# Attention block: query tiles ahead of the maxima on VectorE, sink columns written a step sooner, and W_o's tiles shared out as 12, 12, 18 and 6 matmuls over the last four steps

## The chip, the cores and the metric

The kernel runs on one core of a Trainium2 chip. The metric is the device time of one execution in microseconds. Before the change it is 1058.06 us, the median of three runs (1057.86 to 1059.98).

## What is computed

A two-layer decoder trunk in float32 on one sequence of 512 tokens and width 1024: an S5 layer with its MLP, then one attention layer with its MLP, and a final RMSNorm. The change touches only the attention layer: 16 query heads over 4 shared K/V heads, causal window of 128, and one learned sink logit for each head.

```python
s = einsum(q, k) / sqrt(64);  s = where(band, s, -inf)      # per block of 128 queries, 256 keys
m = maximum(max(s), sink)
p = exp(s - m);  denom = sum(p) + exp(sink - m)
o = einsum(p / denom, v)
h = h + o @ w_o + b_o
```

## The kernel before

There is no scheduler. Each engine has its own instruction stream, written out by hand, and the streams meet only at semaphores. Every dense product is done as three float32r passes (high times high, high times low, low times high): the weights come from HBM as panels of 128x1024 into two buffers `raw`, and GpSimd turns each into `w_hi` (L436) and `w_lo` (L439, which reads `raw` and `w_hi`, both in SBUF). It starts on a panel when the unit three before it is finished on TensorE (`unit_done`, a tiny gating operation at L351). A unit is 8 tiles of 3 matmuls of 128x128 by 128x512 (L1256 to L1258), 24 in all.

Attention is cut into 16 pieces Q = 4u + n: four heads (u) of one block of 128 tokens (n). For n = 0 only half of the window exists, so the pieces 0, 4, 8 and 12 have half the columns. The stages of a piece are skewed over steps by `skewed`: in step S each engine goes through a fixed list.

- TensorE: `scores(S)` (L1387), `mix(S-3)` (L1413), `turn_p(S-2)` (L1399, transposes), and then `dense(S)`: matmuls of W_q or W_o that stand beside the attention. Steps 0 to 10 have half a query unit each (12 matmuls); an even step S finishes query unit 2 + S/2. Steps 11 to 18 have parts of the first four W_o units.
- VectorE: `denominators(S-1)` (a reciprocal of 128x4, L1035), `maxima(S)`, `next_queries(S-1)` (in odd steps: `queries(m)`), `turned(S-2)` (L1040), `o_low(S-3)` (L1046).
- ScalarE: `norm_p(S-1)` (L655), `o_hi(S-3)` (L667), `turned(S-2)` (L661), `exps(S)` (L648, four exponentials, each with a sum).

`maxima(Q)` writes the sink logits into the last column of the scores (L1020, 128x4, SBUF to SBUF), adds the mask to the scores out of PSUM (L1022), takes the maxima (L1028) and negates them (L1030, 128x4, SBUF to SBUF). `queries(m)` takes a finished query unit out of PSUM times `rstd` (L1007) and adds the bias with the scale (L1009, 128x512, SBUF to SBUF). `scores(Q)` waits for `q_done` 2u + 2, so piece 4 waits for query tile 3, piece 8 for tile 5 and piece 12 for tile 7. It also waits for the mask of the piece before (`s_masked`), whose PSUM banks it writes. `exps(Q)` waits for `negm`, `denominators(Q)` for the exponentials, `norm_p(Q)` for the reciprocal, `turn_p(Q)` for `norm_p(Q)`, and `mix(Q)` for both copies `turned(Q)`. `out_unit` waits for `ot_lo`, the end of `o_low`, of the tiles it reads. After step 18, TensorE finishes the first four W_o units (their tiles 6 and 7), does the other four, and goes on to the second MLP.

Of the kernel before, what the change touches and what calls it, by code (L numbers as in the profile page):

```python
# [10 lines left out]
ALU = mybir.AluOpType  # L11
# [22 lines left out]
DEEP = 3  # L34
NQ = 16
NKV = 4
BLK = 128
NBLK = L // BLK
QUADS = 4
# [59 lines left out]
def build(nc, panels, xu_d, x_d, lam_d, turns_d, prm_d, dd_d, cst_d, mask_d, col_d, out_d):  # L99
    ctx = ExitStack()  # L100
    with ctx:
        def sb(name, shape, dt=F32, where=ctx):
            return where.enter_context(nc.sbuf_tensor(name, shape, dt))

        def sem(name):
            return ctx.enter_context(nc.semaphore(name))
# [96 lines left out]
        s_sb = sb("s_sb", [P, DEEP, 4, 2 * BLK + 1], where=over)  # L203
# [33 lines left out]
        stat_col_mm, stat_c, out_rstd = sem("stat_col_mm"), sem("stat_c"), sem("out_rstd")  # L237
        hid_t, hid_sq, hid_hi, hid_lo = sem("hid_t"), sem("hid_sq"), sem("hid_hi"), sem("hid_lo")
        kv_done = sem("kv_done")
        q_done, s_mm, s_masked, m_step = sem("q_done"), sem("s_mm"), sem("s_masked"), sem("m_step")  # L240
        p_exp, rden_done, p_norm = sem("p_exp"), sem("rden_done"), sem("p_norm")
        pt_mm, pt_v, pt_a = sem("pt_mm"), sem("pt_v"), sem("pt_a")
# [3 lines left out]
        def wait(eng, s, value):  # L246

            if not (isinstance(value, int) and value <= 0):
                eng.wait_ge(s, value)
# [9 lines left out]
        def COLS(name):  # L259
            a, b = COL[name]  # L260
            return col[:, a:b]
# [20 lines left out]
        def window(n):  # L282

            return slice(BLK if n == 0 else 0, 2 * BLK)

        def halves_of(n):
            return (1,) if n == 0 else (0, 1)
# [166 lines left out]
        def _(a):  # L454
# [187 lines left out]

            def exps(Q):
                u, n, r = Q // NBLK, Q % NBLK, Q % DEEP
                a.wait_ge(m_step, 3 * Q + 3)
                at = slice(window(n).start, 2 * BLK + 1)
                for j in range(4):
                    act_fn(s_sb[:, r, j, at], s_sb[:, r, j, at], ACT.Exp, bias=negm[:, r, j:j + 1],  # L648
                           accum_out=den[:, r, j:j + 1]).then_inc(p_exp, 1)
# [14 lines left out]
            def o_hi(Q):  # L664
# [4 lines left out]
                       ACT.Copy).then_inc(ot_hi, 1)  # L669

            skewed([(norm_p, 1), (o_hi, 3), (turned, 2), (exps, 0)])

            for m in range(KT):
# [6 lines left out]
        def _(v):  # L680
            tt, ts, stt = nc.vector.tensor_tensor, nc.vector.tensor_scalar, nc.vector.scalar_tensor_tensor
# [332 lines left out]
            wait(v, s_mask, 16)  # L1014


            def maxima(Q):
                u, n, r = Q // NBLK, Q % NBLK, Q % DEEP
                sink = COLS("sink")[:, 4 * u:4 * u + 4]
                ts(s_sb[:, r, :, 2 * BLK:], sink.unsqueeze(2), 1.0, None, ALU.mult).then_inc(m_step, 1)  # L1020
                v.wait_ge(s_mm, Q + 1)
                tt(s_sb[:, r, :, window(n)],  # L1022
                   ps[:, 0:2, :].rearrange("p e (t m) -> p (e t) m", t=2)[:, :, window(n)],
                   mask[:, window(n)].unsqueeze(1).to_broadcast([P, 4, len(halves_of(n)) * BLK]),
                   ALU.add).then_inc(s_masked, 1)
                v.wait_ge(s_masked, Q + 1)
                v.wait_ge(m_step, 3 * Q + 1)
                nc.vector.tensor_reduce(mx[:, r], s_sb[:, r, :, window(n).start:], AX.X, ALU.max).then_inc(m_step, 1)  # L1028
                v.wait_ge(m_step, 3 * Q + 2)
                ts(negm[:, r], mx[:, r], -1.0, None, ALU.mult).then_inc(m_step, 1)  # L1030

            def denominators(Q):
# [18 lines left out]
            def next_queries(Q):  # L1051
                if Q % 2 == 0 and 2 + Q // 2 < KT:
                    queries(2 + Q // 2)

            skewed([(denominators, 1), (maxima, 0), (next_queries, 1), (turned, 2), (o_low, 3)])


            for m in range(KT):
# [12 lines left out]
        def _(pe):  # L1071
# [347 lines left out]
                      for Q in range(2 * (KT - 2) - 1)}  # L1419
            last_quad = QUADS * NBLK - 1  # L1420

            for step, work in ((-4, [(0, 0, 2)]), (-3, [(0, 2, 4)]), (-2, [(1, 0, 2)]), (-1, [(1, 2, 4)]), (0, [(0, 4, 6)]),
                               (1, [(1, 4, 6), (2, 0, 2)]), (2, [(2, 2, 6)]), (3, [(3, 0, 6)])):
                beside[last_quad + step] = [(out_unit, m, range(k, end)) for m, k, end in work]

            def dense(Q):
# [20 lines left out]
def skewed(stages):  # L1447

    last = QUADS * NBLK
    longest = max(lag for _, lag in stages if lag is not None)
    for Q in range(last + longest):
        for stage, lag in stages:
            if lag is None:
                stage(Q)
            elif 0 <= Q - lag < last:
                stage(Q - lag)
# [111 lines left out]
```

## Time and profile before

| | |
|---|---|
| median of three runs | 1058.06 us |
| the profiled execution, its own time | 1057.35 us |
| its span | 1055.3 us |
| TensorE matmul busy | 1026.4 us (97% of the span) |
| VectorE, ScalarE, GpSimd busy | 565.0, 230.4 and 694.6 us |
| mean granted TensorE clock | 0.989 |
| attention steps 0 to 18 | from 569.33 us to about 666.9 us |

The span is from the first to the last instruction of the profiled execution. Busy shares are means over stages that differ; the change lives in the 98 us of the attention steps, so only that stretch is read closely. Step S is taken to begin with `scores(S)` on TensorE (steps 16 to 18 have no scores and begin with `mix`).

### The profile page before, as it was taken

The page shows a single profiled execution, that of the slowest core. Times are in us where ns is not written, and L with a number is a line of the kernel's source. Part 1 is how long each engine was busy: PE and PEld are TensorE (multiplying, and loading weights), DVE is VectorE, ACT ScalarE, POOL GpSimd, SP SyncE. Part 2 cuts the span into 40 slices and gives each one's busy share as a digit, 9 for nine tenths or more (in the row PEclk, how much of TensorE's full clock was granted, in tenths as well). Part 3 has the DMA queues.
Part 4 walks back from the last instruction along what each step waited for, and adds up shares of the span by engine and source line. Part 5 has one row for each costly group of instructions (what it writes and reads, how often), then busy time and mean ns, then how long its engine had stood idle before and what let it go on. Part 6 is the DMA issues. An engine that isn't in the chain of part 4 may idle for free.

```text
span 1055.3 us, 15740 instructions
## 1 busy us (share of the span) xinstructions
PE 1026.4 (97%) x5734; PEld 840.0 (80%) x5734; DVE 565.0 (54%) x661; ACT 230.4 (22%) x512; POOL 694.6 (66%) x568
## 2 busy tenths in 40 slices
PE   8799999999999999999999999999999999999996
PEld 3687888888888888888887677888888888888886
DVE  8894355677316514713855776568761472273125
ACT  7763211211001000101312778221100010010011
POOL 8896876587767766766646230688776676676650
PEclk9799999999999999999999999999999999999999
DMA  6124323232222322333323110232222222223312
GB/s 247 30 42 134 106 100 99 80 103 97 100 99 100 99 93 86 100 99 100 99 80 100 41 41 21 63 118 100 99 100 99 100 96 94 89 99 100 99 61 80
DMA packets 35905, 97.52 MB, mean 92 GB/s; under 512 B 11144, under 2 KB 13704, under 8 KB 35600
## 3 DMA queue, kind: packets, MB, share of 16 engines
q1 hardware_dynamic: 35856, 96.83, 27.7%
q8 instruction: 35, 0.57, 0.2%
q14 instruction: 14, 0.11, 0.0%
HBM read 92.36 MB, written 2.10 MB: 90 GB/s over the span
## 4 chain that ended last, share of the span: by engine, by line
PE 86%; DVE 5%; ACT 3%; issue 2%; SPq 2%; DMA 1%; DVEq 0%; POOL 0%; ACTq 0%; POOLq 0%
PE ps L1256 23%; PE ps L1258 23%; PE ps L1257 23%; PE ps L1212 2%; PE ps L1214 2%; PE ps L1213 2%; SPq L315 2%; ACT s_sb L648 1%; DVE mx L1028 1%; DMA toep<-k_even 1%; PE ps L1413 1%; DVE s_sb L1022 1%; PE ps L1399 1%; PE ps L1319 1%; PE ps L1318 1%
## 5 line engine op out<-in xcount | busy, mean ns | idle before, releaser
L439 POOL TENSOR_TENSOR w_lo<-raw,w_hi 128x1024 fp32r<-128x1024 f32 x164 | 414.8, 2529 | 13.7
L1256 PE MATMUL ps<-hid,w_hi 128*128 128x512 f32 x704 | 275.9, 392 | 0.0
L1258 PE MATMUL ps<-hid,w_lo 128*128 128x512 f32 x704 | 274.0, 389 | 0.0
L1257 PE MATMUL ps<-hid,w_hi 128*128 128x512 f32 x704 | 274.0, 389 | 0.0
L351 POOL TENSOR_TENSOR gate_sb<-gate_sb 128x1 f32<-128x1 f32 x164 | 41.1, 250 | 309.7 <-PE ps L1258 271.0
L1256 PE MATMUL ps<-act,w_hi 128*128 128x512 f32 x464 | 180.6, 389 | 0.0
L1257 PE MATMUL ps<-act,w_hi 128*128 128x512 f32 x464 | 180.5, 389 | 0.0
L1258 PE MATMUL ps<-act,w_lo 128*128 128x512 f32 x464 | 180.5, 389 | 0.0
L436 POOL TENSOR_SCALAR w_hi<-raw 128x1024 fp32r<-128x1024 f32 x164 | 173.1, 1056 | 0.0
L1258 PEld LDWEIGHTS ps<-hid,w_lo 128*128 128x128 f32 x704 | 132.2, 188 | 27.7
L1256 PEld LDWEIGHTS ps<-hid,w_hi 128*128 128x128 f32 x704 | 132.2, 188 | 27.6 <-issue 0.5
L1257 PEld LDWEIGHTS ps<-hid,w_hi 128*128 128x128 f32 x704 | 132.2, 188 | 26.9
L913 DVE TENSOR_TENSOR hid<-t,hid 128x512 fp32r<-128x512 f32 x64 | 129.1, 2018 | 44.8 <-ACT hid L608 44.8
L924 DVE TENSOR_TENSOR h<-ps,h 128x512 f32 x48 | 33.2, 692 | 205.3 <-PE ps L1258 205.3
L608 ACT ACTIVATE hid<-t 128x512 fp32r<-128x512 f32 x64 | 40.5, 633 | 455.6 <-DVE t L911 455.6
L1257 PEld LDWEIGHTS ps<-act,w_hi 128*128 128x128 f32 x464 | 87.1, 188 | 18.2
L1258 PEld LDWEIGHTS ps<-act,w_lo 128*128 128x128 f32 x464 | 87.1, 188 | 18.1
L1256 PEld LDWEIGHTS ps<-act,w_hi 128*128 128x128 f32 x464 | 87.1, 188 | 18.0
L909 DVE SCALAR_TENSOR_TENSOR t<-ps,rstd 128x512 f32<-128x512 f32 x64 | 44.1, 690 | 56.2 <-PE ps L1258 54.7
L911 DVE TENSOR_TENSOR t<-t 128x512 f32<-128x512 f32 x64 | 67.1, 1049 | 2.2
L863 DVE SCALAR_TENSOR_TENSOR act<-h,col,act 128x512 fp32r<-128x512 f32 x24 | 49.5, 2062 | 20.7 <-ACT act L579 20.7
L579 ACT ACTIVATE act<-h,col 128x512 fp32r<-128x512 f32 x24 | 17.4, 724 | 127.6 <-DVE h L933 72.3
(217 smaller groups left out, 1067.5 us busy)
## 6 DMA issues: line engine op xcount, KB each, us to landing
raw<-panels_in SPq DMA_DIRECT2D x164, 512.0 KB, 3.2
xy<-xu_in SPq DMA_DIRECT2D x4, 512.0 KB, 7.6
out<-h SPq DMA_DIRECT2D x8, 256.0 KB, 2.2
prm<-prm_in SPq DMA_DIRECT2D x1, 1280.0 KB, 5.8
h<-x_rows_in SPq DMA_DIRECT2D x1, 1280.0 KB, 12.9
h<-x_rows_in SPq DMA_DIRECT2D x1, 768.0 KB, 7.7
dd<-dd_in SPq DMA_DIRECT2D x1, 256.0 KB, 5.7
toep<-k_even SPq DMA_DIRECT2D x4, 64.0 KB, 2.3
```

What stands on the lines that cost most here:

```text
L351: nc.gpsimd.tensor_tensor(gate_sb[:, 0:1], gate_sb[:, 1:2], gate_sb[:, 1:2], ALU.mult)
L436: nc.gpsimd.tensor_scalar(w_hi[:, s, :], raw[:, s % 2, :], 1.0, 0.0, ALU.mult, ALU.add).then_inc(w_hi_done, 1)
L439: nc.gpsimd.tensor_tensor(w_lo[:, s, :], raw[:, s % 2, :], w_hi[:, s, :].bitcast(F32), ALU.subtract).then_inc(w_split, 1)
L608: act_fn(hid[:, par, 0, m, :], t2[:, m % 2, :], ACT.Copy).then_inc(hid_hi, 1)
L863: stt(dst[:, 1, m, :], h[:, m, :], COLS(g)[:, m:m + 1], dst[:, 0, m, :].bitcast(F32), ALU.mult, ALU.subtract).then_inc(n_lo, 1)
L909: stt(t1[:], ps[:, (m + shift) % 4, :], 0.0, rstd[:], ALU.max, ALU.mult).then_inc(bank_free, 1)
L911: tt(t2[:, m % 2, :], t1[:], t1[:], ALU.mult).then_inc(hid_sq, 1)
L913: tt(hid[:, par, 1, m, :], t2[:, m % 2, :], hid[:, par, 0, m, :].bitcast(F32), ALU.subtract).then_inc(hid_lo, 1)
L924: tt(tile(h, m), ps[:, (s + shift) % 4, :], tile(h, m), ALU.add).then_inc(bank_free, 1)
L1256: mm(ps[:, bank, :], w_hi[:, s, w], x[:, 0, k, :], start=(k == 0), stop=False)
L1257: mm(ps[:, bank, :], w_hi[:, s, w], x[:, 1, k, :], start=False, stop=False)
L1258: last = mm(ps[:, bank, :], w_lo[:, s, w], x[:, 0, k, :], start=False, stop=(k == KT - 1))
```

## The change

Three edits. First, on VectorE `next_queries(S-1)` goes ahead of `maxima(S)` in each step. Second, the sink write is taken out of `maxima` and becomes `sinks_in(Q)`, issued at the end of the step before (with a wait on `pt_mm` for the buffer and a semaphore `sunk` of its own); `m_step` now counts two for each piece. Third, on TensorE the W_o matmuls of steps 15 to 18 are 12, 12, 18 and 6, where they were 6, 12, 12 and 18; steps 11 to 14 keep 6 each. No operation is added or taken away in any of the three.

```diff
-                a.wait_ge(m_step, 3 * Q + 3)
+                a.wait_ge(m_step, 2 * Q + 2)
...
+            def sinks_in(Q):
+
+                wait(v, pt_mm, Q - DEEP + 1)
+                sink = COLS("sink")[:, 4 * (Q // NBLK):4 * (Q // NBLK) + 4]
+                ts(s_sb[:, Q % DEEP, :, 2 * BLK:], sink.unsqueeze(2), 1.0, None, ALU.mult).then_inc(sunk, 1)
+
+            def next_sinks(Q):
+                if Q + 1 < QUADS * NBLK:
+                    sinks_in(Q + 1)
+
             def maxima(Q):
                 u, n, r = Q // NBLK, Q % NBLK, Q % DEEP
-                sink = COLS("sink")[:, 4 * u:4 * u + 4]
-                ts(s_sb[:, r, :, 2 * BLK:], sink.unsqueeze(2), 1.0, None, ALU.mult).then_inc(m_step, 1)
                 v.wait_ge(s_mm, Q + 1)
...
-                v.wait_ge(m_step, 3 * Q + 1)
+                v.wait_ge(sunk, Q + 1)
                 nc.vector.tensor_reduce(mx[:, r], s_sb[:, r, :, window(n).start:], AX.X, ALU.max).then_inc(m_step, 1)
-                v.wait_ge(m_step, 3 * Q + 2)
+                v.wait_ge(m_step, 2 * Q + 1)
                 ts(negm[:, r], mx[:, r], -1.0, None, ALU.mult).then_inc(m_step, 1)
...
-            skewed([(denominators, 1), (maxima, 0), (next_queries, 1), (turned, 2), (o_low, 3)])
+            sinks_in(0)
+            skewed([(denominators, 1), (next_queries, 1), (maxima, 0), (turned, 2), (o_low, 3), (next_sinks, None)])
...
-            for step, work in ((-4, [(0, 0, 2)]), (-3, [(0, 2, 4)]), (-2, [(1, 0, 2)]), (-1, [(1, 2, 4)]), (0, [(0, 4, 6)]),
-                               (1, [(1, 4, 6), (2, 0, 2)]), (2, [(2, 2, 6)]), (3, [(3, 0, 6)])):
+            for step, work in ((-4, [(0, 0, 2)]), (-3, [(0, 2, 4)]), (-2, [(1, 0, 2)]), (-1, [(1, 2, 4)]), (0, [(0, 4, 6), (1, 4, 6)]),
+                               (1, [(2, 0, 4)]), (2, [(2, 4, 6), (3, 0, 4)]), (3, [(3, 4, 6)])):
```

## Rows read from the trace of the kernel before

**Rows 1.** The page's first part: busy us (share of the span) and instructions.

```profile
PE 1026.4 (97%) x5734; PEld 840.0 (80%) x5734; DVE 565.0 (54%) x661; ACT 230.4 (22%) x512; POOL 694.6 (66%) x568
```

**Rows 2.** The chain that ended last, steps 13 and 14: start us, us, what.

```profile
638.82 1.18 DVE s_sb L1022
...
643.83 1.13 DVE s_sb L1022
```

**Rows 3.** Busy time by stretch, step 3: PE, PEld, DVE, ACT, POOL, clock, DMA.

```profile
581.30:589.00 7.70, 5.63 (x39) 4.15 (x38) 5.69 (x11) 5.69 (x19) 3.57 (x3) 1.00 0.20 69
```

**Rows 4.** Timeline of TensorE: start us, us, what [idle before <-releaser].

```profile
576.93 1.13 PE L1387 MATMUL ps<-kT,qT 64*128 64x256 f32 x8
...
581.33 1.13 PE L1387 MATMUL ps<-kT,qT 64*128 64x256 f32 x8
583.24 0.66 PE L1413 MATMUL ps<-pT,v_sb 128*64 128x128 f32 x8 [0.77 <-DVE pT L1040]
...
588.99 0.71 PE L1387 MATMUL ps<-kT,qT 64*128 64x128 f32 x8 [1.30 <-DVE qT L1009]
589.81 1.09 PE L1413 MATMUL ps<-pT,v_sb 128*64 128x128 f32 x16
...
594.63 1.13 PE L1387 MATMUL ps<-kT,qT 64*128 64x256 f32 x8
...
600.52 1.14 PE L1387 MATMUL ps<-kT,qT 64*128 64x256 f32 x8
...
605.93 1.13 PE L1387 MATMUL ps<-kT,qT 64*128 64x256 f32 x8
...
616.85 1.13 PE L1387 MATMUL ps<-kT,qT 64*128 64x256 f32 x8
...
633.36 0.71 PE L1387 MATMUL ps<-kT,qT 64*128 64x128 f32 x8 [1.05 <-DVE qT L1009]
...
652.08 1.09 PE L1413 MATMUL ps<-pT,v_sb 128*64 128x128 f32 x16 [1.78 <-ACT pT L661]
```

**Rows 5.** Timeline of VectorE, from before step 0 to step 5.

```profile
562.07 1.40 DVE L1009 TENSOR_SCALAR qT<-t,col 128x512 f32<-128x512 f32 x1
...
567.51 0.94 DVE L1009 TENSOR_SCALAR qT<-t,col 128x512 f32<-128x512 f32 x1
568.49 2.23 DVE L1020 TENSOR_SCALAR s_sb<-col 128x4 f32<-128x4 f32 x1
...
573.95 0.18 DVE L1035 RECIPROCAL rden<-den 128x4 f32<-128x4 f32 x1 [1.72 <-ACT s_sb L648]
...
574.20 1.21 DVE L1022 TENSOR_TENSOR s_sb<-ps,mask 128x1024 f32<-128x1024 f32 x1
...
576.71 0.17 DVE L1030 TENSOR_SCALAR negm<-mx 128x4 f32<-128x4 f32 x1
...
577.50 0.49 DVE L1009 TENSOR_SCALAR qT<-t,col 128x512 f32<-128x512 f32 x1
...
581.75 1.03 DVE L1030 TENSOR_SCALAR negm<-mx 128x4 f32<-128x4 f32 x1
...
589.96 0.18 DVE L1035 RECIPROCAL rden<-den 128x4 f32<-128x4 f32 x1
...
594.21 0.18 DVE L1035 RECIPROCAL rden<-den 128x4 f32<-128x4 f32 x1 [1.22 <-ACT s_sb L648]
```

**Rows 6.** Timeline of GpSimd, the same stretch.

```profile
560.79 2.40 POOL L439 TENSOR_TENSOR w_lo<-raw,w_hi 128x1024 fp32r<-128x1024 f32 x1
...
568.26 2.43 POOL L439 TENSOR_TENSOR w_lo<-raw,w_hi 128x1024 fp32r<-128x1024 f32 x1
...
574.36 2.41 POOL L439 TENSOR_TENSOR w_lo<-raw,w_hi 128x1024 fp32r<-128x1024 f32 x1
...
581.71 1.05 POOL L436 TENSOR_SCALAR w_hi<-raw 128x1024 fp32r<-128x1024 f32 x1
...
596.06 2.38 POOL L439 TENSOR_TENSOR w_lo<-raw,w_hi 128x1024 fp32r<-128x1024 f32 x1
```

More of the change, by code:

```diff
@@ L239, in build @@
         kv_done = sem("kv_done")
+        sunk = sem("sunk")
         q_done, s_mm, s_masked, m_step = sem("q_done"), sem("s_mm"), sem("s_masked"), sem("m_step")
```

## The prediction

> **What bounds the kernel now.** I began with the page: TensorE's matmuls fill 97% of the span [rows 1], so outside the attention time only goes where TensorE stands still, and whatever the attention steps gain or lose arrives at the end one for one. The view by stretches shows such a place: step 3 has 5.63 us of matmuls in 7.70 us, at a granted clock of 1.00, so a wait of two microseconds has not lowered the clock here [rows 3]. TensorE's timeline then names each wait in steps 0 to 18, 4.90 us in all [rows 4]: 0.77 at mix(0) for VectorE's `turned(0)`, 1.30 at scores(4) for query tile 3, 1.05 at scores(12) for tile 7, and 1.78 at mix(13) for ScalarE's `turned(13)`. Otherwise steps 4 to 10 run at TensorE's own pace (5.89 us for a full step with 12 dense matmuls, 5.41 for one with a half piece). From step 11 on only 6 dense matmuls stand in a step, and the chain that ended last leaves TensorE for the loop mask, maxima, exponentials, reciprocal, mask: 5.01 us a step [rows 2]. So there are two regimes: TensorE paces the middle, the VectorE/ScalarE loop paces steps 11 to 15.
>
> The reader is to see a third thing, which decides this change. Some VectorE operations from SBUF to SBUF last far too long. L1009 takes 0.49 us at 577.50 but 1.40 at 562.07, where GpSimd's L439 (2.40 from 560.79) ends at 563.19: it ended 0.28 after it. The sink write at 568.49 took 2.23 and ended 0.03 after the L439 from 568.26 ended. A `negm` of 128x4 took 1.03 at 581.75 and ended 0.02 after the L436 from 581.71 [rows 5, 6]. A waiting operation can also be let in between: the L1009 of 567.51 ended at 568.45, though an L439 had begun at 568.26. The mask addition and L1007, with one operand in PSUM, show no such stretch. So L1009, sink write and `negm` stand still while GpSimd splits a panel, unless they come before L439. And GpSimd splits a panel exactly when a query unit ends, which is when `queries` becomes due.
>
> **Edit 1: queries ahead of the maxima.** Free, the two operations cost 1.2 us. Before, they stood behind `negm`, covered by the exponentials (about 2.1 us). Now they stand between the reciprocal and the mask, inside the loop: behind them wait mask, maxima, `negm`, and through these the exponentials, both copies `turned`, and the PSUM banks of the next scores. Held, they cost more. I follow it step by step; S with a number is the start of that step on TensorE.
>
> Step 1: reciprocal 573.95, L1009 due 0.8 later (from `negm` over L1007 to L1009 it is 0.79, rows 5) at 574.75. L439 has run since 574.36 and ends at 576.77; so L1009 ends at 577.05 and mask(1) begins at 577.08 instead of 574.20. Its end, 1.21 + 0.05 later, is what scores(2) waits for: S2 = 578.34, against 576.93 (+1.41).
>
> Steps 2 and 3: S3 would be ready 4.40 later, 582.74. mask(2) comes a loop after mask(1), 582.07, and negm(2) 2.51 after that (574.20 to 576.71), 584.58. The split that follows unit 3 has its L436 at S3 + 0.38, its L439 some 1.14 after that: 584.26 to 586.65. So negm(2) meets the L439, not the L436 as before, and ends at 586.68. mix(0) follows 0.46 after it (582.78 to 583.24): 587.14, and S4 4.45 after that (588.99 - 1.30 - 583.24): 591.59. The reciprocal comes 2.2 after negm(2), the queries another 1.2 (free now), then mask(3) at 590.2 and negm(3) at 592.7.
>
> Steps 4 and 5: mix(1) needs `turned(1)`, which comes right behind negm(3); from `negm` to the mix I take 0.90 (0.46, with 0.28 for the full copy, plus `negm`'s own 0.17). mix(1) = 593.6 and S5 = 593.6 + 4.82 (594.63 - 589.81) = 598.4: +3.8. The 1.30 us wait for tile 3 is gone, but it has only become a wait for `turned`.
>
> From here it feeds itself. L439 begins 1.43 after an odd step's start (596.06 - 594.63). The reciprocal before step 5 comes 2.33 + 4.25 after negm(3) (589.96 to 594.21 for the second), 599.3, so L1009 is due at 600.1, 0.25 after L439's 599.85. Held again, mask(5) begins 1.43 + 2.39 + 0.31 = 4.13 after S5, and mix(3) can come 2.51 + 0.90 later, at S5 + 7.54. TensorE would have it at S5 + 5.89 + 1.06 = 6.95: +0.59. In step 7 L1009 is due 1.4 us into L439; TensorE reaches mix(5) at S7 + 6.15 instead of 7.5: +1.35. Step 9 repeats step 5 (due 0.25 into L439), +0.59. S9 = 598.4 + 22.22 + 0.59 + 1.35 = 622.6, against 616.85: +5.7. Step 11: S11 = 622.6 + 11.30 + 0.59 = 634.5, mask(11) from 638.6 to 639.8, S12 = 639.86, against 633.36: +6.5.
>
> Steps 12 to 16 are in the loop's regime. reciprocal(11) is at 638.6 + 4.84 = 643.4, the next 4.25 later, mask(13) at 647.75, against 638.82: +8.93. mix(13) keeps its distance of 13.26 us, less 0.04 twice (edit 2): 660.9, against 652.08: **+8.85**. TensorE itself would be there at 659.5, edit 3's matmuls included, so it is the loop that decides.
>
> **Edit 2: sink writes.** 0.04 to 0.05 us less in each turn of the loop, counted above. At the end of a step they lie under the exponentials (1.1 us room); even held by an L436 they are through before the next reciprocal. Without that cover each would cost up to 2.2 us, as at 568.49; sinks_in(0) keeps its place and its hold.
>
> **Edit 3: 12, 12, 18, 6.** Six matmuls at 0.23 us move ahead of mix(13), where TensorE waits anyway: after mix(13), 1.39 us less are left. `ot_lo` of the tiles they read is long there. In step 18 only 6 matmuls, 1.4 us, now cover o_hi and o_low of the last piece before tiles 6 and 7; these take some 0.9 us. Worth **-1.39**, as long as the wait at mix(13) is 1.4 or more; it was 1.78, and in my sum it is 660.9 - 659.5 = 1.4.
>
> **Sum:** +8.85 - 1.39 = **+7.5 us**. Against the profiled execution, 1057.35, that is 1064.8 (span 1062.8); the median of the runs lies 0.7 above it, so I give 1058.06 + 7.5 = **1065.5**.
>
> What is not in rows is how fast a held operation comes out, when it is held by L439 in the new place; the rows have 0.28 for L1009 and 0.02 to 0.03 for small ones. The Trainium skill (SBUF — State Buffer, section Who interferes with whom) says that the two engines share a port pair under an exclusive lock, and that the one that comes second is blocked for the other's whole instruction. By that, L1009's full 0.49 would follow the release, not 0.28: +0.2 at each of the five odd steps from 1 to 11 that set a wait, about +1 in all, a sum of +8.5. The rows show less, and I stay with them.
>
> **Rivals.**
>
> *The hold lets go on the way.* Three of the meetings are close: negm(2) comes 0.3 us after L439 begins, L1009 in steps 5 and 9 0.25 after. If negm(2) slips in front, 1.9 is saved: +5.6. If L1009 of step 9 slips in front, steps 10 to 12 run as before behind a delay of 5.1 to 5.7: +4.6. If that of step 5 does, +3.8 - 1.4 and 0.4 for the queries in the loop: +2.8. Each estimate of a start is good to about 0.1 to 0.2. I give all of these together 0.27.
>
> *The queries are not held in step 1* (the opposite outcome: not slower). It decides there: L1009 would have to come before 574.36, 0.4 earlier than due, or share the port with L439. Then S2 keeps its time, the wait of 1.30 at scores(4) turns into one of about the same length at mix(1), and at step 11 the queries lengthen the loop by 0.5 to 1.2 as it becomes the bound. With -1.39: between -1.0 and 0, 1057 to 1058. The 562.07 row speaks against it. Chance 0.12.
>
> *The change does what it looks like:* the two waits for query tiles vanish (1.30 + 1.05) and the filler takes 1.39: -3.7, 1054.3. It would need `turned(1)` and `turned(9)` not to slip with their `negm`, though they stand behind it. Chance 0.05.
>
> *Worse:* every hold costs its full length and TensorE's longer waits (up to 2.7 us, where 2.07 in one step was the most before) cost clock: above +9.5. Chance 0.06.
>
> **Chances and range.** The full sum has 0.50, with its own range from +6.5 to +9.5 (1064.5 to 1067.5). With the hold that lets go (from +2.8) it is 0.77; the range is 1060.5 to 1067.5, which takes in the unknowns of release. A measurement of this kernel tells 0.2%, 2.1 us, from no change. Faster by more: 0.05, from the third rival. Within: 0.13, the second and the edge of the first. Slower: 0.82.
>
> **What the changed profile would show.** L1009 at about 574.8, lasting 2.3 us, and mask(1) at 577.1; a wait of 1.4 at scores(2); negm(2) some 2 us long and mix(0) near 587; S5 near 598.4; L1009s of about 2 us in steps 5, 7, 9 and 11; waits of TensorE for L1040 at mix(3), mix(5), mix(7) and mix(9); mix(13) near 660.9; step 17 with 18 dense matmuls and no wait in step 18. If instead L1009 stays at 0.5 us, the step that failed is the hold in step 1. If it is held but S5 is below 597, it was negm(2).

## The result, and the profile after

The changed kernel takes 1065.78 us, the median of 6 runs (1065.18 to 1069.14), against 1058.42 for the kernel before (6 runs). The ratio is 1.0075, with a 95% interval from 1.0064 to 1.0086. That is 7.4 us slower; 7.5 were predicted (1065.5). The span of the profiled execution is 1063.4 us, against 1055.3.

To compare kernels finely, the attention steps are measured in the profile from `scores(0)` to the first addition of W_o to h (L1060 before, L1070 after). The views by stretch over exactly these steps, before and after (columns as in [rows 3]):

```profile
569.33:668.48 99.15, 94.09 (x676) 72.21 (x676) 64.97 (x125) 69.72 (x224) 22.90 (x19) 1.00 0.12 40
```

```profile
569.04:676.57 107.53, 97.14 (x676) 74.74 (x676) 72.88 (x125) 68.98 (x224) 22.83 (x19) 0.97 0.11 37
```

The steps took 99.15 us and take 107.53: +8.38, so the loss sits where it was expected. The same 676 matmuls are busy 3 us longer, at a mean clock of 0.97 instead of 1.00, and TensorE stands still for 10.4 us instead of 5.1. Against [rows 4 to 6] all times here are 0.29 us early, since scores(0) came at 569.04 instead of 569.33.

TensorE's timeline of the changed kernel:

```profile
569.04 0.72 PE L1397 MATMUL ps<-kT,qT 64*128 64x128 f32 x8
...
578.11 1.13 PE L1397 MATMUL ps<-kT,qT 64*128 64x256 f32 x8 [1.40 <-issue]
...
583.01 1.13 PE L1397 MATMUL ps<-kT,qT 64*128 64x256 f32 x8 [0.43 <-issue]
586.85 1.12 PE L1423 MATMUL ps<-pT,v_sb 128*64 128x128 f32 x8 [2.70 <-DVE pT L1049]
...
594.02 0.72 PE L1397 MATMUL ps<-kT,qT 64*128 64x128 f32 x8
...
599.47 1.13 PE L1397 MATMUL ps<-kT,qT 64*128 64x256 f32 x8
...
618.30 1.09 PE L1423 MATMUL ps<-pT,v_sb 128*64 128x128 f32 x16 [1.34 <-issue]
...
623.10 1.14 PE L1397 MATMUL ps<-kT,qT 64*128 64x256 f32 x8
...
630.61 1.09 PE L1423 MATMUL ps<-pT,v_sb 128*64 128x128 f32 x16 [0.48 <-issue]
...
640.51 0.71 PE L1397 MATMUL ps<-kT,qT 64*128 64x128 f32 x8 [1.39 <-issue]
642.56 1.09 PE L1423 MATMUL ps<-pT,v_sb 128*64 128x128 f32 x16 [1.34 <-issue]
...
656.35 0.66 PE L1423 MATMUL ps<-pT,v_sb 128*64 128x128 f32 x8 [0.49 <-issue]
...
661.51 1.09 PE L1423 MATMUL ps<-pT,v_sb 128*64 128x128 f32 x16 [0.74 <-ACT pT L662]
```

The two waits for query tiles of [rows 4] are gone, as the order of the edit suggests. In their place stand waits at scores(2), scores(3) and scores(12), and at mix(0), mix(5), mix(7), mix(9) and mix(12); mix(13) still waits, 0.74 us instead of 1.78. Where the view names only "issue", the stream of TensorE shows what it waits for: the mask of the piece before at the scores, the copy `turned` at a mix.

VectorE's timeline, and GpSimd's (L1010 is L1009 of before, L1022 the sink write, L1039 `negm`, L437 and L440 the former L436 and L439; where the text goes on to speak of L1009 and L439, the operation is meant, whatever its line in that kernel):

```profile
573.64 0.18 DVE L1044 RECIPROCAL rden<-den 128x4 f32<-128x4 f32 x1 [1.65 <-ACT s_sb L649]
...
574.43 2.33 DVE L1010 TENSOR_SCALAR qT<-t,col 128x512 f32<-128x512 f32 x1
576.79 1.22 DVE L1031 TENSOR_TENSOR s_sb<-ps,mask 128x1024 f32<-128x1024 f32 x1
...
584.20 2.17 DVE L1039 TENSOR_SCALAR negm<-mx 128x4 f32<-128x4 f32 x1
...
600.31 0.80 DVE L1010 TENSOR_SCALAR qT<-t,col 128x512 f32<-128x512 f32 x1
...
612.18 2.70 DVE L1010 TENSOR_SCALAR qT<-t,col 128x512 f32<-128x512 f32 x1
...
624.79 2.40 DVE L1010 TENSOR_SCALAR qT<-t,col 128x512 f32<-128x512 f32 x1
...
637.75 1.39 DVE L1010 TENSOR_SCALAR qT<-t,col 128x512 f32<-128x512 f32 x1
```

```profile
574.07 2.40 POOL L440 TENSOR_TENSOR w_lo<-raw,w_hi 128x1024 fp32r<-128x1024 f32 x1
...
584.01 2.34 POOL L440 TENSOR_TENSOR w_lo<-raw,w_hi 128x1024 fp32r<-128x1024 f32 x1
...
599.78 1.05 POOL L437 TENSOR_SCALAR w_hi<-raw 128x1024 fp32r<-128x1024 f32 x1
600.91 2.42 POOL L440 TENSOR_TENSOR w_lo<-raw,w_hi 128x1024 fp32r<-128x1024 f32 x1
...
612.21 2.39 POOL L440 TENSOR_TENSOR w_lo<-raw,w_hi 128x1024 fp32r<-128x1024 f32 x1
...
624.53 2.38 POOL L440 TENSOR_TENSOR w_lo<-raw,w_hi 128x1024 fp32r<-128x1024 f32 x1
...
636.48 2.38 POOL L440 TENSOR_TENSOR w_lo<-raw,w_hi 128x1024 fp32r<-128x1024 f32 x1
```

Read them side by side. Four of the six L1010 end 0.28 to 0.29 us after an L440 ends (576.76 after 576.47, 614.88 after 614.60, 627.19 after 626.91, 639.14 after 638.86). The one at 600.31 was held too, but by the shorter first operation: it ended at 601.11, 0.28 after the L437 of 599.78, and so it got in between this and the L440 of 600.91, and took 0.80. The sixth, in step 3, met no split and took 0.49. `negm` at 584.20 lasted until 586.37, 0.02 after the L440 of 584.01.

Steps 3 and 4 by stretch show one thing more:

```profile
583.00:586.80 3.80, 1.13 (x8) 0.74 (x8) 3.74 (x4) 1.20 (x4) 3.26 (x2) 0.90 0.00 0
586.80:594.00 7.20, 7.15 (x28) 5.70 (x28) 4.87 (x9) 5.58 (x20) 0.00 (x0) 0.58 0.20 74
```

TensorE had stood still since 584.15. Within this wait the granted clock fell:

```profile
586.00:586.40 0.40, 0.00 (x0) 0.00 (x0) 0.40 (x2) 0.00 (x0) 0.35 (x1) 0.58 0.00 0
586.40:586.80 0.40, 0.00 (x0) 0.00 (x0) 0.38 (x2) 0.39 (x1) 0.00 (x0) 0.50 0.00 0
```

It is 0.58 on average over the next 7.2 us, most of which TensorE ran at the lower of its two levels (1.2 GHz), and step 3 took 7.17 us from mix(0) to scores(4) instead of the 4.45 it needs at 2.4 GHz.

### The profile page after: what moved, and what is told of

Read it like the earlier page. It is cut to its first block, busy times and chain, and to the rows that moved or that the text cites. A ratio compares the mean times of both kernels' runs of the same rounds, so it can differ in the third digit from the quotient of the medians.

```text
span 1063.4 us, 15740 instructions
## 1 busy us (share of the span) xinstructions
PE 1029.8 (97%) x5734; PEld 842.8 (79%) x5734; DVE 572.6 (54%) x661; ACT 229.5 (22%) x512; POOL 693.0 (65%) x568
## 4 chain that ended last, share of the span: by engine, by line
PE 85%; DVE 8%; issue 3%; ACT 3%; SPq 0%; DMA 0%; DVEq 0%; POOL 0%; ACTq 0%; POOLq 0%
PE ps L1266 23%; PE ps L1268 23%; PE ps L1267 23%; PE ps L1222 2%; PE ps L1224 2%; PE ps L1223 2%; ACT s_sb L649 1%; PE ps L1423 1%; DVE qT L1010 1%; PE ps L1409 1%; DVE mx L1037 1%; DVE s_sb L1031 1%; PE ps L1329 1%; PE ps L1328 1%; PE ps L1327 1%
## 5 line engine op out<-in xcount | busy, mean ns | idle before, releaser
L440 POOL TENSOR_TENSOR w_lo<-raw,w_hi 128x1024 fp32r<-128x1024 f32 x164 | 414.4, 2527 | 13.7
L437 POOL TENSOR_SCALAR w_hi<-raw 128x1024 fp32r<-128x1024 f32 x164 | 172.1, 1050 | 0.0
```

What stands on the lines that cost most here:

```text
L437: nc.gpsimd.tensor_scalar(w_hi[:, s, :], raw[:, s % 2, :], 1.0, 0.0, ALU.mult, ALU.add).then_inc(w_hi_done, 1)
L440: nc.gpsimd.tensor_tensor(w_lo[:, s, :], raw[:, s % 2, :], w_hi[:, s, :].bitcast(F32), ALU.subtract).then_inc(w_split, 1)
```

## The experiments

Ten kernels ran. "Steps" is the length of the attention steps in the profile, and "to S5" the part of it up to scores(5). Ratios are to the kernel before on the same chip, with 4 to 12 runs of each new kernel and 10 to 29 of the kernel before. S5 is the start of scores(5).

| kernel | median, us | ratio (95%) | steps, us | to S5 | from S5 |
|---|---|---|---|---|---|
| before | 1058.42 | | 99.15 | 25.30 | 73.85 |
| changed | 1065.78 | 1.0075 (1.0064 to 1.0086) | 107.53 | 30.43 | 77.10 |
| e1, edit 1 alone | 1068.94 | 1.0102 (1.0085 to 1.0120) | 109.86 | 30.38 | 79.48 |
| e2, edit 2 alone | 1057.17 | 0.9988 (0.9978 to 0.9998) | 97.68 | 24.07 | 73.61 |
| e3, edit 3 alone | 1056.86 | 0.9984 (0.9973 to 0.9994) | 97.78 | 25.28 | 72.50 |
| e4, changed, L1009 reads PSUM | 1060.02 | 1.0017 (1.0006 to 1.0028) | 101.98 | 28.76 | 73.22 |
| e5, e4 without `negm` | 1056.55 | 0.9980 (0.9968 to 0.9992) | 97.76 | 25.55 | 72.21 |
| e6, changed without `negm` | 1061.92 | 1.0043 (1.0025 to 1.0060) | 102.86 | 26.61 | 76.25 |
| e7, step 1 as before | 1061.29 | 1.0025 (1.0015 to 1.0036) | 102.09 | 24.46 | 77.63 |
| e8, edits 2 and 3, no `negm` | 1053.32 | 0.9955 (0.9941 to 0.9969) | 95.13 | 23.46 | 71.67 |
| e9, changed, wait filled | 1065.62 | 1.0070 (1.0055 to 1.0086) | 107.24 | 29.12 | 78.12 |
| e10, edits 2 and 3 | 1054.75 | 0.9968 (0.9956 to 0.9981) | 96.35 | 24.08 | 72.27 |

**One edit at a time.** e1 is the kernel before with a new order on VectorE:

```diff
-            skewed([(denominators, 1), (maxima, 0), (next_queries, 1), (turned, 2), (o_low, 3)])
+            skewed([(denominators, 1), (next_queries, 1), (maxima, 0), (turned, 2), (o_low, 3)])
```

> Edit 1 alone on the kernel before. Theory (held queries): the whole loss is here. The changed kernel's attention steps, from scores(0) to the first addition of W_o to h, are 107.53 us against 99.15; without edit 3 they should be 1.39 longer still, and 0.1 to 0.8 longer for the sink write that stands in the loop again: 109.0 to 109.7, time +9.5 to +10.5 us. L1009 is again held in step 1 (2.3 us). Rival (the new shares of W_o or the moved sink writes cost the time): at most +2 us, and the loss shows in e2 or e3.

Measured: 109.86 us of steps, +10.7, a little over the theory's upper end; L1009 of step 1 took 2.28 us. The whole loss is in edit 1. In step 5, where L1009 got in before L439, the sink write behind it, which here still stands in the loop, was held instead:

```profile
601.34 2.22 DVE L1020 TENSOR_SCALAR s_sb<-col 128x4 f32<-128x4 f32 x1
```

The clock fell twice here, at the wait of mix(0) as in the changed kernel, and again after those at scores(12) and mix(9), where the changed kernel's profile keeps 1.00:

```profile
643.20:647.00 3.80, 3.76 (x27) 3.32 (x28) 2.50 (x8) 3.56 (x12) 0.00 (x0) 0.62 0.01 2
```

e2 has only `sinks_in`, with the queries behind the maxima.

> Edit 2 alone. Theory: 0.04 to 0.05 us less in each turn of the loop, and the held sink writes of steps 7 and 11 (0.68 and 0.76 us before) leave the way to the mask: attention steps 98.4 to 99.1 us, time -0.1 to -0.8 us, not to be told from zero. Rival: the early sink write is held by the splits at the end of even steps and comes in the way of the next reciprocal: +0.5 us or more for each such step.

Measured: 97.68 us, -1.47, twice the most that was expected. The rows of e2's VectorE and GpSimd show why:

```profile
582.24 0.17 DVE L1039 TENSOR_SCALAR negm<-mx 128x4 f32<-128x4 f32 x1
582.32 0.42 DVE L1049 TENSOR_SCALAR pT<-ps 128x256 f32<-128x256 f32 x1
582.42 1.04 POOL L437 TENSOR_SCALAR w_hi<-raw 128x1024 fp32r<-128x1024 f32 x1
582.65 0.84 DVE L1022 TENSOR_SCALAR s_sb<-col 128x4 f32<-128x4 f32 x1
```

Before, negm(2) met GpSimd's first operation and took 1.03 us [rows 5]. Here it comes 0.22 us earlier, counted from scores(0), and ends 0.01 before that operation starts at 582.42. The hold falls on the sink write behind it (0.84), where the exponentials cover it: no wait at mix(0), and 0.91 instead of 1.30 at scores(4), which makes S4 1.22 us earlier; the other 0.25 of the 1.47 come in the later steps.

e3 has only the new shares of W_o.

> Edit 3 alone. Theory: six matmuls move into the wait of 1.78 us at mix(13), so attention steps 97.8 us (99.15 less 1.39) and time -1.4 us; the wait at mix(13) shrinks to 0.4 us. Rival: the short step 18 uncovers o_hi and o_low of the last piece, and tile 6 waits for ot_lo: the gain is given back, 0 us.

Measured: 97.78 us, -1.37. The wait at mix(13), 1.78 before, is

```profile
654.19 1.06 PE L1413 MATMUL ps<-pT,v_sb 128*64 128x128 f32 x15 [0.41 <-issue]
```

0.41 us, and nothing waits in step 18. Theory met.

**Is it the hold?** e4 takes the hold from the query operations, not by time but by where they read:

```diff
-                tt(t1[:], ps[:, query_bank(m), :], rstd[:], ALU.mult).then_inc(bank_free, 1)
-                v.wait_ge(bank_free, 4 + U_Q + 1 + m)
-                ts(qT[:, m, :], t1[:], COLS("b_q")[:, m:m + 1], HD ** -0.5, ALU.add, ALU.mult).then_inc(q_done, 1)
+                bank = ps[:, query_bank(m), :]
+                tt(bank, bank, rstd[:], ALU.mult).then_inc(q_scaled, 1)
+                v.wait_ge(q_scaled, m + 1)
+                ts(qT[:, m, :], bank, COLS("b_q")[:, m:m + 1], HD ** -0.5, ALU.add, ALU.mult).then_inc(q_done, 1)
                 v.wait_ge(q_done, m + 1)
+                v.sem_inc(bank_free, 1)
```

> The changed kernel, with the product of a query tile and rstd written back to its PSUM bank instead of an SBUF tile, so that the bias operation reads PSUM (0.69 us instead of 0.49) and has no SBUF input beside the bias column. Theory (it is GpSimd's hold that costs): no query operation is longer than 0.7 us, mask(1) begins 1.45 us after the reciprocal, S5 returns to within 0.3 us of before, attention steps 98.0 to 99.2 us, time -1.2 to 0 us against before, 8 to 9 us under the changed kernel. Rival (the order itself costs, 1.45 us in each of six turns of the loop): the attention steps stay at 106 us or more.

Measured: 101.98 us, 5.5 under the changed kernel, but 2.8 over the upper end of the theory. No query operation took more than 0.75 us. What was left out of the sum is the second of these rows:

```profile
582.77 2.34 POOL L441 TENSOR_TENSOR w_lo<-raw,w_hi 128x1024 fp32r<-128x1024 f32 x1
582.89 2.25 DVE L1042 TENSOR_SCALAR negm<-mx 128x4 f32<-128x4 f32 x1
```

GpSimd's second operation had begun at 582.77. By 0.12 us negm(2) fell behind it, mix(0) waited 2.78 us, and the clock fell to 0.59 as in the changed kernel. From S5 on the steps take 73.22 us, 3.9 less than in the changed kernel. So the hold of L1009 is shown, and a second place of the same kind. No run took GpSimd's splits away; that it is they that hold rests on this run and on the ends: in all twelve profiles, every L1009 that is held ends 0.27 to 0.30 us after a split operation, and every held operation of 128x4 0.02 to 0.04 after one.

e5 does the negation inside the reduction as well:

```diff
-                nc.vector.tensor_reduce(mx[:, r], s_sb[:, r, :, window(n).start:], AX.X, ALU.max).then_inc(m_step, 1)
-                v.wait_ge(m_step, 2 * Q + 1)
-                ts(negm[:, r], mx[:, r], -1.0, None, ALU.mult).then_inc(m_step, 1)
+                nc.vector.tensor_reduce(negm[:, r], s_sb[:, r, :, window(n).start:], AX.X, ALU.max,
+                                        negate=True).then_inc(m_step, 1)
```

> The kernel of e4 (changed kernel, bias operation reading PSUM), and the negation done inside the reduction, so that the loop has neither L1009 nor negm on the side that GpSimd can hold. Theory (in e4 what is left of the loss is negm(2) held for 2.25 us and the lower clock after the long wait): the wait at mix(0) falls from 2.78 to under 1 us, the clock stays at 1.00 in steps 3 and 4, S5 comes within 0.5 us of before, attention steps 97.4 to 98.8 us against 101.98 in e4 and 99.15 before; time -0.5 to -1.8 us. Rival (the order of e4 costs its loss through the loop alone): 101 us or more.

Measured: 97.76 us, the wait at mix(0) 0.50, S5 0.25 later than before. Theory met. With nothing in the loop that can be held, the new order is no longer slower than the kernel before. It isn't better than the old order either, as e8 will show. Its mix(1) has the wait that scores(4) had before, and scores(4) still waits 0.62:

```profile
591.46 0.77 PE L1425 MATMUL ps<-pT,v_sb 128*64 128x128 f32 x10 [1.19 <-DVE pT L1051]
```

**Which hold does what?** e6 is the changed kernel with e5's reduction only.

> The changed kernel with only the negation done inside the reduction; L1009 can still be held. Theory: mask(1) still begins 2.9 us late, but turned(0) is not held behind negm(2), so the wait at mix(0) falls to about 0.7 us and the clock does not fall. Step 5 then depends on L1009's race with L439: if it is held, the later steps lose as in the prediction, attention steps 104 to 106.5 us; if it slips in front, 102 to 104. Rival (the first hold, not negm, makes the 2.7 us wait and all that follows): 107 us as in the changed kernel.

Measured: 102.86 us. The wait at mix(0) is 0.50, and the clock is 1.00 in the stretches of steps 3 and 4. L1010 of step 5 was held (2.46 us), yet the total came out in the range meant for the case that it slips in front. Both parts were put too high: S5 comes 26.61 us after scores(0), only 1.31 later than before, and the waits at mix(3), mix(5), mix(7) and mix(9) are 0.28, 1.14, 0.29 and 1.14, each 0.2 shorter than in e7, which still has `negm`.

e7 leaves query tile 2 behind the maxima in step 1:

```diff
+            def ahead(Q):
+                if Q > 0:
+                    next_queries(Q)
+
+            def behind(Q):
+                if Q == 0:
+                    next_queries(Q)
+
-            skewed([(denominators, 1), (next_queries, 1), (maxima, 0), (turned, 2), (o_low, 3), (next_sinks, None)])
+            skewed([(denominators, 1), (ahead, 1), (maxima, 0), (behind, 1), (turned, 2), (o_low, 3), (next_sinks, None)])
```

> The changed kernel, with query tile 2 behind the maxima in step 1 alone, as before; tiles 3 to 7 stay ahead. Theory (the first hold starts it): S2 at its old time, negm(2) as in e2, S5 within 0.5 us of before, L1009 slips in front of L439 in steps 5, 9 and 11 and has a race within 0.03 us in step 7: attention steps 98 to 99.5 us if it wins there, about 102 to 104 if it loses. Rival (each step is held by itself): 105 us or more.

Measured: 102.09 us. S5 is 0.84 earlier than before (24.46), but from there on it is as bad as the changed kernel, 77.63. The theory that the first hold starts the others fell with these rows of step 5:

```profile
597.75 2.38 POOL L440 TENSOR_TENSOR w_lo<-raw,w_hi 128x1024 fp32r<-128x1024 f32 x1
...
597.95 2.47 DVE L1010 TENSOR_SCALAR qT<-t,col 128x512 f32<-128x512 f32 x1
```

In steps 7, 9 and 11 L1010 took 1.33, 2.40 and 1.40. The reason lies in the order: mix(1) waits for `turned(1)` (1.38 us in e7), and from then on both S5, which sets GpSimd off, and the reciprocal, which sets L1010 off, hang on the same `negm`. Their distance is fixed, whatever came before: in e6, e7 and e9, the three kernels with a wait at mix(1) and an L1009 that can be held, L1010 of step 5 begins 0.20, 0.20 and 0.19 us after L440. The first hold, negm(2) and the clock cost about 6 us up to S5 (30.43 against 24.46). From S5 on the order costs its own 4.8 to 5.4: 77.10 in the changed kernel and 77.63 in e7, against 72.27 in e10, which has the same edits 2 and 3 and the old order (the kernel before, with 73.85, has neither).

**The clock.** e9 adds ten matmuls, whose result isn't used, to the wait at mix(0):

```diff
+                if Q == 0:
+                    for _ in range(10):
+                        mm(ps[:, 7, :], minus[:], hid[:, 0, 0, 0, :], start=True, stop=True)
                 pe.wait_ge(pt_a, Q + 1)
                 pe.wait_ge(pt_v, Q + 1)
```

> The changed kernel with ten extra matmuls of 128x512 (their result is not used) between scores(3) and mix(0), in the wait of 2.70 us, so that TensorE has little idle time there. Theory (the lower clock after the wait cost time): the granted clock stays at 1.00 through steps 3 and 4, S5 lies 29.0 to 29.3 us after scores(0) instead of 30.43. L1009 of step 5 then comes 0.2 to 0.3 us after L439 has begun, is held for more than 2 us, and gives back 0.5 us: attention steps 106 to 107.2 us against 107.53. Rival (the clock would have fallen anyway, or its loss lies under the wait for turned(1)): S5 at 30.2 us or later.

Measured: S5 after 29.12 us, 1.31 earlier than in the changed kernel, and the stretches keep the full clock:

```profile
583.00:586.80 3.80, 3.39 (x19) 2.45 (x18) 3.73 (x3) 1.50 (x5) 3.27 (x3) 1.00 0.00 0
586.80:594.00 7.20, 5.63 (x39) 4.08 (x37) 5.31 (x11) 5.21 (x17) 0.32 (x1) 1.00 0.23 74
```

Then L1010 of step 5, which came 0.19 after L440's start, was held for 2.47 us, and mix(3) waited 0.48, which the late S5 had avoided in the changed kernel. The steps are 107.24 long, 0.04 over the theory's end. At scores(12) 0.70 of the 1.31 are left. More of it went on a second fall of the clock, after the waits of 1.41 at scores(12) and 1.34 at mix(9):

```profile
642.56:647.59 5.03, 5.03 (x31) 4.06 (x31) 3.02 (x9) 4.78 (x17) 0.00 (x0) 0.66 0.00 2
```

The same stretch from mix(9) to scores(13) takes 3.44 us at full clock in the changed kernel. So the fall in step 3 costs 1.31 us up to S5, but e9 does not show that the total would be 1.3 shorter without it: it was 0.3.

**A better version.** e10 has edits 2 and 3 and leaves the queries behind the maxima; e8 has the negating reduction too. For both the order is

```diff
-            skewed([(denominators, 1), (next_queries, 1), (maxima, 0), (turned, 2), (o_low, 3), (next_sinks, None)])
+            skewed([(denominators, 1), (maxima, 0), (next_queries, 1), (turned, 2), (o_low, 3), (next_sinks, None)])
```

> A candidate: edits 2 and 3, the negation inside the reduction, and the queries behind the maxima as before. Theory: e2 had 97.68 us and e3 takes 1.37 off where TensorE waits at mix(13); without negm each turn of the loop is about 0.1 us shorter: attention steps 95.3 to 96.5 us, time -2.7 to -4.0 us. Rival (the waits for tiles 3 and 7 grow by what the loop gives up, and the filler finds no wait to fill): 97 us or more.

> Edits 2 and 3 together, the queries behind the maxima as before, negm kept. Theory (e2 and e3 add up): attention steps 96.2 to 96.5 us, time -2.5 to -3 us, so that of e8's gain of 4.0 us some 1.1 come from the negation inside the reduction. Rival (they use the same wait at mix(13)): 97 us or more.

Measured: e10 96.35 us of steps and a ratio of 0.9968 (edits 2 and 3 add up: -1.47 - 1.37 would be 96.31); e8 95.13 us and 0.9955, 1053.32 us. In the view by stretch e8's steps show

```profile
569.35:664.48 95.13, 93.97 (x676) 72.16 (x676) 60.53 (x108) 69.25 (x224) 22.94 (x19) 1.00 0.13 42
```

so TensorE stands still for 1.2 us of 95, 0.30 of it at scores(4) and 0.71 at scores(12). Both beat the kernel before and the changed one. e8 against e5 (95.13 against 97.76) bounds the price of the queries in the loop when nothing is held. The two differ in the order and in where L1009 reads, which takes 0.75 us from PSUM and 0.49 from SBUF. Of the 2.63 us, the slower read can explain at most six times 0.26, that is 1.6, so the order costs at least 1.0. No run has the one without the other.

## Why the prediction was right

Times are given from scores(0), predicted against measured in the changed kernel.

- **Step 1.** scores(2) at 9.01 against 9.07, with a wait of 1.40 where 1.41 was predicted. Right.
- **negm(2) behind the second split operation.** mix(0) at 17.81 against 17.81. Right; e4, e5 and e6 confirm that it is `negm`'s hold that makes this wait.
- **S5.** 29.1 against 30.43. Here the forecast missed 1.3 us: the clock fell in the wait at mix(0). The prediction had the clock only as part of the rival "worse". It had taken from [rows 3] that a wait of two microseconds had not lowered the clock; but these were two waits, of 0.77 and 1.30 us, and no row of before has a single one of 2.70. e9 shows the price, 1.31 us.
- **L1009 held in step 5.** Wrong in the changed kernel (0.80 us, no wait at mix(3)): with the late S5, L1009 waited for the end of its query unit (0.41 us before L1008), met L437 and got in before L440. It was right at full clock (e9) and in e6 and e7. Of the 1.3 us from the clock, the missing wait at mix(3) gives 0.6 back.
- **Steps 7, 9 and 11.** Waits at mix(5) 1.35 against 1.34, mix(7) 0.59 against 0.48. For scores(12) and mix(9) the prediction names no wait; its times leave about 1.2 and 1.3 us, and 1.39 and 1.34 were measured. The mechanism is right in each. In step 7 the margin wasn't what was expected: L1010 was due 1.4 us into L440 and came at the very moment of its start (in e7 and e9, where step 5 was held, it came 1.34 into it). The wait is the same either way, since L440's end sets it.
- **mix(13).** 91.6 against 92.5, so +9.7 where +8.85 was predicted; S7 and S9 were already 0.8 over the forecast, so this is what was left at S7 of the miss at S5.
- **Edit 2.** In steps 13 to 15 a turn of the loop, mask to mask, takes 4.90 us instead of 4.97: 0.07 less, where 0.04 to 0.05 were predicted. Alone it is worth 1.47: the prediction had no term for what a shift of 0.2 us does at negm(2).
- **Edit 3.** -1.39 predicted; e3 measures -1.37. In the changed kernel, with the moved matmuls ahead of it, the wait left at mix(13) is 0.74, not the 1.4 of the prediction; 0.49 more lie at mix(12).
- **The sum.** +7.5 predicted; the steps show +8.4, the medians +7.4. The steps are 0.9 longer than predicted, the 0.9 of mix(13). The 1 us between steps and medians comes from two places. Scores(0) comes 0.29 earlier in the profile of the changed kernel (after the steps both profiles take 386.8 us to their end), so the profiled executions differ by 8.05 (1065.40 less 1057.35). And the median of the kernel before lies 1.07 above its profiled execution, that of the changed kernel 0.38, within the scatter of the runs (1057.07 to 1059.98 for the kernel before). So the agreement within 0.1 us is luck: a forecast 0.9 too low for the steps met a difference of medians 1.0 lower than that of the steps. The mechanism is right without it.

On the port: the Trainium skill (SBUF — State Buffer, section Who interferes with whom) gives an exclusive lock for the whole instruction. The rows agree on who waits for whom: L1010 from SBUF was held, from PSUM (e4) not. But a released L1010 ended 0.28 us after, not its full 0.49, so the sum by the rows was the better one. That the sum by the Trainium skill, +8.5, lies nearer to the +8.4 of the steps is chance: most of what the steps have above +7.5 is what the fall of the clock left over (0.8 of 0.9 at S7).

The rival that the edit does what it looks like (-3.7) fails on mix(1): in e5, with nothing held, TensorE still waits there for 1.19 us. The rival without a hold (-1.0 to 0) supposed the queries free and `negm` kept. That is e4's case, and there negm(2) was held all the same: the steps are 2.8 longer than before, and the ratio is 1.0017. Only with `negm` out as well, in e5, are they 1.4 shorter. The rival "the hold lets go" had its condition met, since L1009 of step 5 slipped in front, but its price of +2.8 was wrong: step 7 was held again, and so were 9 and 11.

## What to carry to other kernels

Before an operation is moved ahead in an engine's order, ask what it then stands in front of, and what else is set off by the event that makes it ready: here the end of a query unit starts both the query operations on VectorE and the split on GpSimd, and the first stand still while the second runs. A short operation from SBUF to SBUF in a loop (a negation of four columns) can cost two microseconds; it is worth folding it into its neighbour or letting it read PSUM, which was tried on L1009 alone. Moving filler work into the stretch that waits paid its length (1.37 of 1.39 us), and where waits differ by tenths of a microsecond from a collision, one profile of each variant tells more than a sum.

## What was not expected of the hardware

- In a wait of TensorE of 2.70 us (2.78 in e4) the granted clock fell, and it was 0.58 (0.59) on average over the 7 us that followed. Two waits at scores(12) and mix(9), 0.7 us apart, were followed by a fall in e1 (1.47 and 1.34 us) and e9 (1.41 and 1.34), to 0.62 and 0.66 on average, and by none in the changed kernel (1.39 and 1.34), e7 (1.40 and 1.34) and e6 (1.42 and 1.14). Single waits of 1.30 and 1.78 us in the kernel before were followed by none, nor was the place at mix(0) in e9, with ten matmuls in it. What decides between the two outcomes at step 12 stays open.
- An operation's recorded start doesn't tell which of the two goes first: L1010 at 612.18 is recorded 0.03 us before the L440 of 612.21, and still ended 0.28 us after it.
- A held L1009 ends 0.27 to 0.30 us after the split operation in every case, though it lasts 0.49 when free; operations of 128x4 end 0.02 to 0.04 after it.
- GpSimd loses next to nothing in these meetings: the L440 of 600.91 began while L1010 was on record until 601.11, and took 2.42 us, where those that hold an L1010 take 2.38 to 2.40.
